# One inverse root per group of row tiles in the bridges between layer parts, with one operand in PSUM

## The reference

```python
def _layernorm(x, g=None, b=None):
    mu = xf.mean(-1, keepdims=True)
    var = jnp.square(xf - mu).mean(-1, keepdims=True)
    y = (xf - mu) * lax.rsqrt(var + LN_EPS)
    ...
x = _layernorm(DEEPNORM_ALPHA * x + g1 * y, ln1_g[l], ln1_b[l])
f = _swiglu(_modulate(_layernorm(x), sh2, sc2), w_gu[l], w_down[l])
x = _layernorm(DEEPNORM_ALPHA * x + g2 * f, ln2_g[l], ln2_b[l])
```

## Time and profile before

| | |
|---|---|
| median of 3 runs | 2493.85 us (2493.56 to 2496.89) |
| the profiled execution: time, and its span from first to last instruction | 2498.33 us, 2496.5 us |
| TensorE busy | 2315.2 us, 93% of the span |
| VectorE, ScalarE, GpSimd busy | 49%, 38%, 44% |
| mean granted TensorE clock | 0.978 |
| VectorE's inverse roots: 42 tiles | 20 first norms, 22 second norms |

### The profile page before, as it was taken

One profiled execution on the slowest core, in us unless ns is written; L12 is line 12 of the kernel. 1 busy time (PEld: TensorE's weight loads), 2 busy tenths in 40 slices (PEclk: granted clock), 3 DMA queues, 4 the chain that ended last, 5 costly groups with the idle time before them and its releaser, 6 DMA issues. The chain is left out here.

```text
span 2496.5 us, 34770 instructions
## 1 busy us (share of the span) xinstructions
PE 2315.2 (93%) x13090; PEld 2107.2 (84%) x13090; DVE 1222.7 (49%) x2548; ACT 949.3 (38%) x1852; POOL 1088.3 (44%) x844
## 2 busy tenths in 40 slices
PE   6989999998899989999999979899998898999997
PEld 2879888987789989999999868778877788988887
DVE  5786266565543474663831274546635526311124
ACT  3222366435541562111111244256535536422223
POOL 1333255434443544333532433446434456644545
PEclk9989999999999999999999989999999999999999
DMA  6541100132112535443522533121222245533335
GB/s 244 193 139 51 51 26 26 43 137 58 58 45 74 181 130 190 134 154 107 171 90 67 161 101 122 54 64 35 65 67 66 66 152 161 152 94 99 110 117 170
DMA packets 117935, 263.86 MB, mean 106 GB/s; under 512 B 13348, under 2 KB 13604, under 8 KB 116136
## 3 DMA queue, kind: packets, MB, share of 16 engines
q1 hardware_dynamic: 108000, 233.89, 29.6%
q10 hardware_dynamic: 9800, 28.19, 3.4%
HBM read 251.53 MB, written 10.49 MB: 105 GB/s over the span
## 5 line engine op out<-in xcount | busy, mean ns | idle before, releaser
L513 POOL TENSOR_TENSOR w_lo<-raw,w_hi 128x512 fp32r<-128x512 f32 x632 | 864.8, 1390 | 1031.2 <-ACT w_hi L587 1030.6
L587 ACT ACTIVATE w_hi<-raw 128x512 fp32r<-128x512 f32 x632 | 366.8, 626 | 682.8 <-PE ps L1747 251.1
L525 POOL TENSOR_TENSOR p_sb<-p_sb,row_inv 128x768 f32<-128x768 f32 (+2 forms) x160 | 185.3, 1168 | 300.7 <-DVE row_inv L1486 300.0
L1745 PE MATMUL ps<-h_hi,w_lo 128*128 128x384 f32 (+1 forms) x864 | 311.4, 360 | 1.2 <-DVE h_lo L1244 1.2
L1745 PE MATMUL ps<-h_lo,w_hi 128*128 128x384 f32 (+1 forms) x864 | 311.1, 360 | 0.0
L1745 PE MATMUL ps<-h_hi,w_hi 128*128 128x384 f32 (+1 forms) x864 | 311.1, 360 | 0.0
L1576 DVE TENSOR_TENSOR ps<-silu_g,ps 128x768 f32<-128x768 f32 (+3 forms) x52 | 37.8, 726 | 379.4 <-PE ps L1747 177.5
L1745 PEld LDWEIGHTS ps<-h_hi,w_lo 128*128 128x128 f32 x864 | 162.2, 188 | 17.3 <-DVE h_lo L1244 1.4
L1745 PEld LDWEIGHTS ps<-h_lo,w_hi 128*128 128x128 f32 x864 | 162.2, 188 | 16.0
L1745 PEld LDWEIGHTS ps<-h_hi,w_hi 128*128 128x128 f32 x864 | 162.2, 188 | 15.9
L2091 PE MATMUL ps<-h_hi,w_lo 128*128 128x384 f32 (+1 forms) x408 | 134.3, 364 | 27.1 <-DVE k_ll L1431 14.8
(11 more groups left out here) (219 smaller groups left out, 5474.4 us busy)
## 6 DMA issues: line engine op xcount, KB each, us to landing
raw<-in_stream SPq DMA_DIRECT2D x632, 256.0 KB, 2.8
ada_raw_gate_up<-in_w_ada SPq DMA_DIRECT2D x48, 512.0 KB, 3.6
ada_raw_fourier_in<-in_w_ada SPq DMA_DIRECT2D x24, 512.0 KB, 4.4
bias_sb<-in_bias ACTq DMA_DIRECT2D x32, 320.0 KB, 3.0
first_raw<-in_w_first SPq DMA_DIRECT2D x8, 1152.0 KB, 5.2
scratch<-xr ACTq DMA_DIRECT2D x16, 512.0 KB, 3.8
xr<-scratch SPq DMA_DIRECT2D x14, 512.0 KB, 4.9
ln_rows<-in_norm_rows SPq DMA_DIRECT2D x8, 512.0 KB, 5.2
```

The costliest lines, as they stand in the source:

```text
L513: nc.gpsimd.tensor_tensor(w_lo[:, u % 2, cols], raw[:, u % 2, cols], w_hi[:, u % 2, cols].bitcast(F32), ALU.subtract).then_inc(S("lo_made" ...
L525: nc.gpsimd.tensor_tensor(p, p, row_inv[:, c:c + 1].broadcast_to([P, keys]), ALU.mult).then_inc(S("p_ready"), 1)
L587: nc.scalar.activation(w_hi[:, s, cols], raw[:, s, cols], ACT.Copy).then_inc(S("hi_made"), 1)
L1745: last = nc.tensor.matmul(bank(0), tile, x[:, k, 0:split], start=start, stop=stop)
```

## The change

1. `inverse_root` per tile becomes `roots` per group: one chain over the 2 to 4 columns of the group. It waits for the squares of all tiles of the group. The variance, the seed's helper and a copy of the root lie in PSUM bank 3 (`ROOT_BANK`), so that each instruction reads at most one operand from SBUF. A first norm takes 15 instructions, a second one 17, whatever the number of tiles.
2. `scale` no longer waits for a root: in `affine` all tiles but the last are scaled ahead of `roots`, the last one between the first two shifts. `produced(1, k)` and `consumed(0, 0)` move to named points between.
3. ACT's places move: for 4 tiles squares at 4, 5 and 6 and `applied` at 6; for 3 tiles squares at 2 and 3, `applied` at 5; for 2 tiles squares at 3 (3 and 4 in group 1 of a lead), `applied` at 5; `store` and `modulated` at 6.
4. The lead's units turn over banks 0 to 2 (`lead_bank`). With that the gate unit of chunk n waits for chunk n - 2 to be split by DVE (`hidden_lo`) and the up unit for chunk n - 1's silu; before, the gate unit waited for the silu and the up unit for `hidden_lo` of chunk n - 2.
5. Tile 3 of the next layer's first token unit lies in bank 3 and waits for the roots.
6. The first norm runs one chain of 13 instructions over six columns, with all operands in SBUF.

```diff
-            def inverse_root(ph, g, second, i):
+            def roots(ph, g, second):
...
+                tmp, root = tmp_s[:, a:a + n], inv_s[:, a:a + n]
+                var_p, tmp_p, root_p = (ps[:, ROOT_BANK, 8 * x:8 * x + n] for x in range(3))
+                dve.wait_ge(S("squared"), at(ph, "squared") + (2 - last) * len(ph.groups[0]) * g + n * second + n)
+                step(nc.vector.tensor_scalar(var_p, square_s[:, second, t:t + n], 1.0 / D, EPS, ALU.mult, ALU.add))
+                step(nc.vector.tensor_scalar(tmp_p.bitcast(I32), var_p.bitcast(I32), 1, None, ALU.logical_shift_right))
+                step(*(nc.vector.tensor_scalar(x.bitcast(I32), tmp_p.bitcast(I32), -1.0, ROOT_SEED, ALU.mult, ALU.add) for x in (root, root_p)))
                 for turn in range(3):
-                    step(nc.vector.tensor_scalar(tmp, root, root, var, ALU.mult, ALU.mult))
-                    step(nc.vector.tensor_scalar(root, tmp, -3.0 * scale * scale, root, ALU.add, ALU.mult))
+                    step(nc.vector.scalar_tensor_tensor(tmp, root, -0.5, root_p, ALU.mult, ALU.mult))
+                    step(nc.vector.tensor_tensor(tmp, tmp, var_p, ALU.mult))
+                    got = nc.vector.scalar_tensor_tensor(root, tmp, 1.5, root_p, ALU.add, ALU.mult)
+                    if turn < 2 or second:
+                        step(got, nc.vector.scalar_tensor_tensor(root_p, tmp, 1.5, root_p, ALU.add, ALU.mult))
                 if second:
+                    got = nc.vector.tensor_tensor(shift_s[:, t:t + n], neg_mean[:, 1, t:t + n], root_p, ALU.mult)
...
-                inverse_root(ph, g, 0, 0)
-                scale(0)
-                for i in range(1, len(tiles)):
-                    inverse_root(ph, g, 0, i)
+                for i in range(n - 1):
                     scale(i)
-                    shift(i - 1)
...
+                    then(("scaled", i))
+                roots(ph, g, 0)
+                then("rooted")
+                shift(0)
+                scale(n - 1)
+                tile_mean(0)
+                then(("shifted", 0))
+                for i in range(1, n):
+                    shift(i)
+                    if i > 1:
+                        tile_mean(i - 1)
+                    then(("shifted", i))
+                tile_mean(n - 1)
...
+                if len(ph.groups[0]) > 2:
+                    affine(ph, 0, works(produced, 1, {("scaled", 0): (1,), ("scaled", 2): (2,), "rooted": (3, 4), ("shifted", 0): (5,),
+                                                      ("shifted", 3): (6,)}))
+                else:
+                    affine(ph, 0, works(produced, 1, {"rooted": (1, 2), ("shifted", 0): (3,), ("shifted", 1): (4, 5, 6)}))
...
+def lead_bank(g, n):
+
+    return (2 * KD + 2 * LEAD * g + n) % PRODUCT_BANKS
```

More of the change, by code:

```diff
@@ L1009, in consumed, with norm_work @@
                     unit_done(u, n % 2, use)
+                def norm_work(g, n):
+                    tiles = len(ph.groups[g])
+                    steps = {4: ((4, 0, 1), (5, 1, 2), (6, 2, 4)), 3: ((2, 0, 1), (3, 1, 3)),
+                             2: ((3, 0, 1), (4, 1, 2)) if g and lead else ((3, 0, 2),)}[tiles]
+                    if n == 0:
+                        squares(ph, g, 0)
+                    for step, first, end in steps:
+                        if n == step:
+                            squares(ph, g, 1, slice(first, end))
+                    if n == (6 if tiles > 3 else 5):
+                        applied(ph, g)
+                    if n == 6:
+                        store(ph, g)
+                        for j in range(KD):
+                            modulated(ph, g, j)
                 if lead:
@@ L1019, in bridge @@
                     produced(1, k)
[L1020 to L1023 removed]
+                    if ends(ph):
+                        if k == 0:
+                            squares(ph, 0, 0)
+                        elif k == KD - 3:
                             store(ph, 0)
[L1025 to L1035 removed]
+                    else:
+                        norm_work(0, k)
                 if ends(ph):
@@ L1041, in bridge @@
                         consumed(0, n)
-                        if n == 0:
-                            squares(ph, 1, 0)
-                        elif n == 2 and len(ph.groups[1]) > 2:
-                            squares(ph, 1, 1, slice(0, 1))
-                        elif n == 3:
-                            squares(ph, 1, 1, slice(len(ph.groups[1]) > 2, None))
-                        elif n == 4:
-                            applied(ph, 1)
-                        elif n == 5:
-                            store(ph, 1)
-                        elif n == 6:
-                            for j in range(KD):
-                                modulated(ph, 1, j)
+                        norm_work(1, n)
                     for n in range(2 * LEAD):
@@ L1128, in chain, with step @@
                 count = [start]
-                def step(instruction):
-                    count[0] += 1
-                    instruction.then_inc(S(name), 1)
+                def step(*instructions):
+                    for instruction in instructions:
+                        count[0] += 1
+                        instruction.then_inc(S(name), 1)
                     dve.wait_ge(S(name), count[0])
@@ new lines, in roots @@
+                n, t = len(tiles), tiles[0]
+                step = chain("norm_step", at(ph, "norm_step") + (FIRST_ROOT + SECOND_ROOT * (not last)) * g + FIRST_ROOT * second)
+                a = ALLT * second + t
+                tmp, root = tmp_s[:, a:a + n], inv_s[:, a:a + n]
+                var_p, tmp_p, root_p = (ps[:, ROOT_BANK, 8 * x:8 * x + n] for x in range(3))
+                dve.wait_ge(S("squared"), at(ph, "squared") + (2 - last) * len(ph.groups[0]) * g + n * second + n)
+                step(nc.vector.tensor_scalar(var_p, square_s[:, second, t:t + n], 1.0 / D, EPS, ALU.mult, ALU.add))
@@ L1164, in inverse_root @@
                 if second:
-                    step(got)
-                    got = nc.vector.tensor_scalar(shift_s[:, t:t + 1], neg_mean[:, 1, t:t + 1], inv, None, ALU.mult)
+                    got = nc.vector.tensor_tensor(shift_s[:, t:t + n], neg_mean[:, 1, t:t + n], root_p, ALU.mult)
                 got.then_inc(S("root_ready"), 1)
-                dve.wait_ge(S("root_ready"), at(ph, "root_ready") + count + 1)
-            def second_roots(ph, g):
-                for i in range(len(ph.groups[g])):
-                    inverse_root(ph, g, 1, i)
+                dve.wait_ge(S("root_ready"), at(ph, "root_ready") + (2 - last) * g + second + 1)
@@ L1190, in added, with affine, then @@
                 tile_mean(len(tiles) - 1)
-            def affine(ph, g, between=()):
+            def affine(ph, g, works={}):
                 tiles, base = ph.groups[g], len(ph.groups[0]) * g
+                n = len(tiles)
                 dve.wait_ge(S("rows_loaded"), at(ph, "rows_loaded") + 32)
+                def then(point):
+                    for work in works.get(point, ()):
+                        work()
                 def scale(i):
@@ L1606, in consumed, with works @@
                     dve.wait_ge(S("unit_done"), ph.unit + 2 * KD + 2 * LEAD * g + 2 * c + 2)
-                    chunk_of_hidden(ph, c, c % 2, LEAD * g + c, a, b, LEAD_BANKS[c % 2][1], False)
+                    chunk_of_hidden(ph, c, c % 2, LEAD * g + c, a, b, lead_bank(g, 2 * c + 1), False)
+                def works(of, g, points):
+                    return {point: [lambda k=k: of(g, k) for k in some] for point, some in points.items()}
                 if lead:
@@ L1615, in bridge @@
                     added(ph, 1)
-                    consumed(0, 0)
-                    affine(ph, 1)
+                    affine(ph, 1, works(consumed, 0, {"rooted": (0,)}))
                     consumed(0, 1)
-                    second_roots(ph, 1)
+                    roots(ph, 1, 1)
                     applied(ph, 1)
```

100 lines of the change are left out of this document (34 added, 66 removed).

## The result

| | before | changed |
|---|---|---|
| time, median of 4 runs each on one chip | 2494.49 us (2493.56 to 2496.89) | 2453.93 us (2452.85 to 2456.52) |
| ratio of the changed kernel to before | | 0.9836, 95% interval 0.9822 to 0.985 |
| profiled execution: time, span | 2498.33, 2496.5 us | 2452.85, 2451.1 us |
| mean granted TensorE clock | 0.978 | 0.986 |

The forecast was 2455; the kernel is 40.6 us faster. The profiled executions differ by 45.4 us, because the one of before took 4 us more than its median.

The account below looks back on a forecast made before the run. The bound was taken to be DVE and ACT alternating over a group, with PE standing still at the bridges; 10.7 + 1.9 + 7.8 + 10.6 + 2.3 + 5.4 = 38.7 us off 2498.3 gave 2459.6, 2455 in the median, range 2447 to 2476.

Parts of the forecast that it names:

- (0,0): Bridge (0,0): waits for ACT in group 0 and the w_lo stall in group 1 go; 1.9 and 7.8 us gained.
- (0,1): Bridge (0,1): turning starts earlier, PE's waits become one of about 10 us ahead of it; 10.7 us gained.
- (1,0): Bridge (1,0): raw weights come earlier in group 0, stalls shrink in both groups; 6.4 + 4.2 = 10.6 us gained.
- First norm: Start of the kernel: one chain of 2.8 us replaces six, so turning ends earlier; 5.4 us gained.
- (1,1): Bridge (1,1) and the end, where the whole tail is the path: shorter chain and passes; 2.3 us gained.
- Half of it: Rival: ACT and DVE wait for each other at `applied`, five moments 3 us late; 15 to 20 us less gain, 2473; chance 0.20.
- PSUM makes each small step slower: Rival for the chains: 60 ns more per instruction, 1.8 us a group, 8.1 us in all: 2463; chance 0.12, within the forecast's.
- Slower or nothing: Rival: the chains' wide integer steps stay dear, 7.2 us a group: 2494, or 2502 at maxima; chances nothing 0.03, slower 0.04.
- The sign that was to show it: In the profile after, integer steps of the chains near 1 us would make the forecast wrong; about 0.16 us was expected.
- Edits at nothing: Bank turnover and tile 3 of the token units waiting for the roots: no gain counted; tile 3 costs 0 to 0.3 us.

Follow-up runs that it names:

- the second profile: The changed kernel run again without an edit, as base beside a later kernel on the same chip: 2454.34 us, ratio to before 0.9838.
- experiment 7: Changed kernel with the stores of the new x for groups of two and three tiles issued right behind applied, as before the change: 2457.49 us, ratio 0.9838.
- experiment 1: Changed kernel with the variance, the helper and the copy of the root in SBUF instead of PSUM: 2487.92 us, ratio to before 0.9972.
- the one comparison made side by side: experiment 10 against the unedited changed kernel on one chip, five runs each: 2447.80 to 2449.39 us against 2453.32 to 2454.86.
- experiment 3: Changed kernel with one chain per group and the new banks, but the old order on VectorE and ScalarE's old places: 2472.55 us, ratio to before 0.9897.
- experiment 10: Changed kernel; for four tiles, units 4 to 6 added later, ScalarE's second squares together, each mean right behind its shift: 2448.45 us, ratio to before 0.9815.

## Why the prediction was right

The step that carried it, one chain for a group instead of one for each tile, came out a little below its price: 2.5 us where 2.7 was worked out and 2.85 taken, 2.8 us where it was 3.0 and 3.2. The places where the time was to come back were the right ones, and the sum of 38.7 us stands against 40.6 in the medians. PE's waits and its granted clock, before and changed, show in which form it came back:

| | (0,0) | (0,1) | (1,0) |
|---|---|---|---|
| sum of PE's waits in the bridge, us | 10.95, 2.20 | 17.78, 10.21 | 12.31, 4.51 |
| mean granted clock in the bridge | 0.98, 1.00 | 0.90, 0.95 | 0.94, 1.00 |

By the prediction's own terms:

- **First norm**, 5.4: 5.55. Turning began at 50.59 where the working said 49.95; the 0.6 us came back between there and the first product, since the first 24 turning products took 4.35 us before, with a granted clock of 0.55 from 51 to 58 us, and 2.81 now, at 1.00.
- **(0,0)**, 9.7: 10.9. All of the 9.5 us of waits on w_lo and acc went, and with new waits of 0.8 us set against them PE waits 8.75 us less, where the working had counted 7.8 (2.4 less 0.5, and 5.9). The other 2.15 us are work that no longer runs at the low clock; 1.9 were counted. ACT's mean was late by 0.73 us, as the lack of slack had let expect.
- **(0,1)**, 10.7: 12.3. From the bridge's start to the turned columns 11.7 us were gained (90.99 to 79.31). Unit 4 was added 63.4 us after the start and not 64.1, and the second chain was 0.4 shorter than taken, against a shift that met GpSimd for 0.6 where I had taken 0.2; some 0.3 us are spread over the rest. That the first chain was shorter gave nothing here, since DVE waited for unit 4 behind it. Another 0.6 came behind the turn. The one stall of about 10 us was forecast; it is 9.3.
- **(1,0)**, 10.6: 12.3, and 11.4 in the second profile. The wait for `applied` ahead of the turned columns is 0.8 us, not 1.3 to 1.8. ACT waited 0.94 us for the raw weights and not 3.22, as counted; experiment 7 bears this out. PE's waits fell by 7.8 us, and the remaining 4.5 us came with the clock, for which the working names 2.3 us in group 1 and no number in group 0.
- **(1,1)**, 2.3: 2.8. The one chain on its path took 2.5 us for the 2.85 taken.

Each of the terms in the bridges is 0.5 to 1.7 us low, all to the same side: I had taken the chains 0.35 to 0.4 us too long each, in (0,0) too few of the waits, and in (1,0) too little of the work as done at the low clock. Why the profiled execution of before took 4 us over its median is not settled. The terms are differences of such executions, and these differ by 45.4 us (43.8 of it in the table) and not by 40.6: against them the sum is 6.7 us low. That the forecast of 2455 came within 1.1 us of the median is therefore in part luck.

**The rivals.** "Half of it" needed 3 us of waiting at five moments; there were 0.7, 1.6 and 1.2 us for second norms' means and 0.8 us ahead of the turned columns in (1,0), and it did not come. ACT's one longer wait for a mean in a bridge, 8.3 us ahead of the first norm's squares of group 1 in (1,1), was 8.2 us before too. "PSUM makes each small step slower" is refuted: 0.15 to 0.17 us a step with a PSUM operand, and the same in SBUF where nothing holds it (experiment 1). The rule of the Trainium skill ("VectorE: DVE Perf Modes", The TRN2 errata), 120 fixed cycles from PSUM against 58, does not show in any of these rows.

"Slower or nothing" was the case to fear, and experiment 1 is that case: with the operands in SBUF the chains of the bridges lose what the grouping gives, and 7 us of 41 remain, about the first norm's. The sign that was to show it, integer steps near 1 us, is there, but it is not the integer steps alone: only 6 of the 42 held steps are integer steps. I had argued from the earlier trace rows that the wide integer steps were dear because GpSimd worked beside them, and that steps on PSUM were free of it. Both parts are now shown. The argument took one sentence in the prediction, and the whole result hung on it. The chances of 0.03 for nothing and 0.04 for slower were right only as long as the change kept one operand of every step in PSUM.

The Trainium skill ("SBUF — State Buffer", Who interferes with whom) says that a VectorE instruction with two SBUF inputs contends with a GpSimd instruction that reads SBUF, and one with at most one SBUF input outside the two-port modes does not. The runs agree: the products of two SBUF operands took 333, 348 and 359 ns on average, and none of the 99 steps with one input in PSUM that began beside GpSimd took over 160. It also says that a two-port copy does, and the held copies of 2 to 4 columns (393 to 522 ns on average) agree.

**Edits at nothing.** No wait of PE on the new bank order is over 0.6 us. I did not run the old bank order with the new chains: bank 3 has to be free of products while the roots lie in it. So what the bank order costs or gives by itself is not shown. The roots in bank 3 cost the next layer's first token units nothing: PE has no wait in the 24 us behind (0,1).

## What to carry to other kernels

Before many small dependent steps are fused over more columns, look at their operands. One-column steps with per-partition scalars were never held here: in the bridges of the kernel before, 182 of 376 began beside a GpSimd subtraction, and none took over 278 ns, as long as they take alone. The same arithmetic over two or more columns, or with two tensors from SBUF, waits out the GpSimd instruction beside which it begins, up to 1.3 us a step. One of two inputs in PSUM keeps such a chain at 0.16 us a step; an output there does not, if both inputs are in SBUF. All of this was seen beside one kind of GpSimd instruction, the subtraction of two SBUF tiles.

A shorter chain pays fully only if the work around it is ordered anew: grouping alone gave 20 us in the bridges, the new order alone nothing, both together 35. Afterwards ask the timeline again for the last wait on the path: moves of a few lines took another 3.6 us out of one bridge. In the one comparison made side by side the time fell by 5.9 us, more than the trace explains.

## What the runs showed of the hardware

- A held step lasts until GpSimd's current instruction ends: four steps of 1.14 to 1.30 us beside four instructions of 1.26 us. An instruction issued directly behind it without a wait takes 0.15 us (2047.58), but the next dependent one, 0.2 us later, is held again if GpSimd has started anew (2047.77).
- The copy of 3 columns is held (430 ns on average) like those of 2 and 4, the copy of 1 column never in 84 instances, 16 of which began beside a GpSimd instruction.
- With two inputs in SBUF a step is held whether its output lies in SBUF or PSUM (348 and 359 ns on average). With one input and the output in PSUM it was not held in 19 steps that began beside GpSimd (at most 165 ns); with the output in SBUF the same step took 0.83 and 0.97 us there (experiment 1).
- The 128x1024 passes suffer from it as well: a shift over two SBUF operands took 1.89 us for 1.27 in the changed kernel and 2.30 in experiment 3, and the two passes of `applied` 3.16 us for 1.53 in experiment 10.
